# Compressed keys and values of a sparse attention: blocks stationary with 256 weight columns moving and a transpose of the result, instead of weight blocks stationary with 64 block columns moving

## The reference, cut to what matters

```python
def compress_blocks(t, tok, pos, w1, w2):
    B, _, G, dh = t.shape
    n_cmp, L = tok.shape
    blocks = t[:, tok] + pos[:, None, :].astype(t.dtype)
    flat = blocks.transpose(0, 1, 3, 2, 4).reshape(B, n_cmp, G, L * dh)
    return jax.nn.gelu(flat @ w1) @ w2
...
    n_cmp = (S - A_CMP_LEN) // A_CMP_STRIDE + 1
    tok = np.arange(n_cmp)[:, None] * A_CMP_STRIDE + np.arange(A_CMP_LEN)[None, :]
    k_cmp = compress_blocks(kc, tok, pos_k, w1_k, w2_k)
    v_cmp = compress_blocks(vc, tok, pos_v, w1_v, w2_v)
```

## Time and profile before

| | |
|---|---|
| median of 3 runs | 4209.5 us (4209.12 to 4214.65) |
| the profiled execution: its own time | 4212.07 us |
| its span in the profile | 4210.2 us |
| TensorE busy | 3891.7 us, 92% |
| VectorE busy | 2173.4 us, 52% |
| ScalarE busy | 1492.2 us, 35% |
| mean granted clock of TensorE | 0.962 |

### The profile page before, as it was taken

How to read it: one execution, slowest core, us unless ns; L and a number is a source line. 1 busy time by engine, 2 the same in 40 slices (tenths; PEclk the granted TensorE clock), 3 DMA queues, 4 the chain that set the end, 5 groups by cost and what they waited for, 6 DMA issues and landing times.

```text
span 4210.2 us, 52635 instructions
## 1 busy us (share of the span) xinstructions
PE 3891.7 (92%) x22400; PEld 3104.3 (74%) x22400; DVE 2173.4 (52%) x3113; ACT 1492.2 (35%) x2571; POOL 134.0 (3%) x160
## 2 busy tenths in 40 slices
PE   7978889879799999999988899999999979999998
PEld 4668658767587688787876687888777757878886
DVE  3764445464543447476545544534564555454346
ACT  3532223223422234343254523322433544232233
POOL 0122100010000000000000000000000000000000
PEclk8989999889899999999999999999999989999999
DMA  3100112103131122322300133333232001332322
GB/s 116 65 7 3 42 50 90 65 21 100 60 120 55 64 96 84 93 90 87 103 18 1 31 96 93 100 95 94 85 105 75 1 16 51 94 97 89 103 91 80
DMA packets 90815, 297.57 MB, mean 71 GB/s; under 512 B 10067, under 2 KB 12627, under 8 KB 90196
## 3 DMA queue, kind: packets, MB, share of 16 engines
q1 hardware_dynamic: 88704, 286.50, 21.4%
q10 hardware_dynamic: 1876, 7.71, 0.5%
HBM read 292.07 MB, written 2.10 MB: 70 GB/s over the span
## 4 chain that ended last, share of the span: by engine, by line
PE 78%; DVE 14%; ACT 5%; issue 2%; POOL 1%; DMA 0%; ACTq 0%; DVEq 0%
PE ps L616 19%; PE ps L617 19%; PE ps L618 19%; PE ps L1131 3%; PE ps L1153 3%; DVE wlo L1913 2%; ACT whi L1277 2%; PE ps L1144 2%; DVE ftm L1944 1%; PE ps L754 1%; PE ps L747 1%; PE ps L651 1%; PE ps L652 1%; PE ps L653 1%; PE ps L759 1%
## 5 line engine op out<-in xcount | busy, mean ns | idle before, releaser
L1913 DVE TENSOR_TENSOR wlo<-wraw,whi 128x1024 fp32r<-128x1024 f32 (+5 forms) x603 | 664.4, 1103 | 1434.1 <-ACT whi L1277 1429.2
L1277 ACT ACTIVATE whi<-wraw 128x1024 fp32r<-128x1024 f32 (+5 forms) x603 | 578.0, 959 | 1455.1 <-PE ps L618 1347.0
L616 PE MATMUL ps<-HH,whi 128*128 128x512 f32 x1816 | 724.0, 399 | 33.2 <-DVE wlo L1913 18.6
L617 PE MATMUL ps<-HL,whi 128*128 128x512 f32 x1816 | 710.7, 391 | 0.0
L618 PE MATMUL ps<-HH,wlo 128*128 128x512 f32 x1816 | 710.1, 391 | 0.0
L616 PEld LDWEIGHTS ps<-HH,whi 128*128 128x128 f32 x1816 | 343.0, 189 | 118.7 <-issue 25.3
L617 PEld LDWEIGHTS ps<-HL,whi 128*128 128x128 f32 x1816 | 343.1, 189 | 76.3 <-issue 6.3
L618 PEld LDWEIGHTS ps<-HH,wlo 128*128 128x128 f32 x1816 | 342.8, 189 | 72.8
L616 PE MATMUL ps<-HBh,whi 128*128 128x512 f32 x752 | 299.1, 398 | 6.9 <-DVE HBl L2414 6.4
L617 PE MATMUL ps<-HBl,whi 128*128 128x512 f32 x752 | 294.1, 391 | 0.0
L618 PE MATMUL ps<-HBh,wlo 128*128 128x512 f32 x752 | 293.6, 390 | 0.0
(11 more groups left out here) (604 smaller groups left out, 6731.4 us busy)
## 6 DMA issues: line engine op xcount, KB each, us to landing
wraw<-in_w_ff SPq DMA_DIRECT2D x88, 512.0 KB, 3.5
wraw<-in_w_bg SPq DMA_DIRECT2D x48, 512.0 KB, 3.5
wraw<-in_ffn_up SPq DMA_DIRECT2D x44, 512.0 KB, 3.3
wraw<-in_w_z SPq DMA_DIRECT2D x36, 512.0 KB, 3.3
wraw<-in_w_gate SPq DMA_DIRECT2D x32, 512.0 KB, 3.3
wraw<-in_w_br SPq DMA_DIRECT2D x32, 512.0 KB, 3.3
wraw<-in_w_rw SPq DMA_DIRECT2D x26, 512.0 KB, 3.3
wraw<-in_w_mam SPq DMA_DIRECT2D x24, 512.0 KB, 3.3
```

The costliest lines, as they stand in the source:

```text
L616: MM(b[0:m, :], hi[:, k, c0:c0 + m], x[0], start=(start and k == 0), stop=False)
L617: MM(b[0:m, :], hi[:, k, c0:c0 + m], x[1], start=False, stop=False)
L1277: ACTV(W.pair_of(n)[0], W.raw_of(n), ACT.Copy).then_inc(*up("act", "whi", n))
L1913: TT(l, W.raw_of(n), h.bitcast(F32), SUB).then_inc(*up("dve", "wlo", n))
```

## The change

The first product of the compression turns round. A piece of `KBh` or `KBl` is now the stationary operand and the 256 columns of a slot row of `w1` move, so a unit is 12 matmuls of 256 columns in place of 24 of 64 columns. A stationary piece is 128 columns wide, twice a slice of before: it takes in the next one as well, and the result rows 64 to 127 are not used. For that, the buffers get 64 more columns (1088). One PSUM bank collects the sum. It holds the hidden values with the blocks on 64 partitions, which is the wrong way round for the product with `w2`. So the GELU goes to a new tile `HT` (64x256), TensorE transposes it with two instructions in a step of its own, and ScalarE copies the result to `HD`. The steps per `n` are now 7 instead of 6, and the places where they come change from `j % 3` to `j % 5`: behind tiles 2, 3, 4, 6, 7, 8, 9, 11, 12, 13, 14, 16 and 17, and the last one after the loop.

```diff
@@ buffers
-                        KBp = (sb(c4, "KBh", 1024, dt=F32R), sb(c4, "KBl", 1024, dt=F32R))
-                        HD, W2 = sb(c4, "HD", 128), sb(c4, "W2", 256)
+                        KBp = (sb(c4, "KBh", 1088, dt=F32R), sb(c4, "KBl", 1088, dt=F32R))
+                        HT, HD, W2 = sb(c4, "HT", 256, 64), sb(c4, "HD", 128), sb(c4, "W2", 256)
@@
-        KBx = [YS[:, 0:1024], YSB[:, 0:1024]]
-        KB4x = [x.rearrange("p (l g n) -> p l g n", l=16, g=2) for x in KBx]
+        KBx = [YS[:, 0:1088], YSB[:, 0:1088]]
+        KB4x = [x[:, 0:1024].rearrange("p (l g n) -> p l g n", l=16, g=2) for x in KBx]
@@ compress, TensorE
-                    acc = [bank("kc", l, n, jt, hold=True) for jt in range(2)]
+                    acc = bank("kc", l, n, hold=True)
                     for lg in range(4):
                         w = W.take(("kc", l, n, lg), "w1" + "kv"[n], (l, lg), 4)
                         hi, lo = W.views(w)
                         for s in due("pe", ("dve", "wlo", w), ("dve", "kb", l, n)):
                             pe.wait_ge(*s)
-                        for jt in range(2):
-                            a = acc[jt]
-                            js = slice(128 * jt, 128 * jt + 128)
-                            for l4 in range(4):
-                                ks_ = slice(64 * (4 * lg + l4), 64 * (4 * lg + l4) + 64)
-                                first, end = lg == 0 and l4 == 0, lg == 3 and l4 == 3
-                                MM(a[:, 0:64], hi[:, l4, js], KBp[0][:, ks_], start=first, stop=False)
-                                MM(a[:, 0:64], hi[:, l4, js], KBp[1][:, ks_], start=False, stop=False)
-                                ins = MM(a[:, 0:64], lo[:, l4, js], KBp[0][:, ks_], start=False, stop=end)
-                            ins.then_inc(*up("pe", "kc", l, n, lg, jt))
+                        for l4 in range(4):
+                            k = slice(64 * (4 * lg + l4), 64 * (4 * lg + l4) + 128)
+                            first, end = lg == 0 and l4 == 0, lg == 3 and l4 == 3
+                            MM(acc[:, 0:256], KBp[0][:, k], hi[:, l4, :], start=first, stop=False)
+                            MM(acc[:, 0:256], KBp[1][:, k], hi[:, l4, :], start=False, stop=False)
+                            ins = MM(acc[:, 0:256], KBp[0][:, k], lo[:, l4, :], start=False, stop=end)
+                        ins.then_inc(*up("pe", "kc", l, n, lg))
                         here("pe", "w", w)
                         if lg < 3:
                             yield
-                    PS.let("kc", l, n, 0)
-                    PS.let("kc", l, n, 1)
+                    here("pe", "kc", l, n)
+                    PS.let("kc", l, n)
+                    yield
+                    b = bank("kct", l, n)
+                    for s in due("pe", ("act", "ht", l, n)):
+                        pe.wait_ge(*s)
+                    for jt in range(2):
+                        ins = TR(b[:, 64 * jt:64 * jt + 64], HT[:, 128 * jt:128 * jt + 128], C("ident")[0:64, 0:64])
+                    ins.then_inc(*up("pe", "kct", l, n))
                     yield
                     b = bank("kc2", l, n)
-                            hd = HD[:, 64 * g + 32 * jt:64 * g + 32 * jt + 31]
+                            hd = HD[:, 64 * jt + 32 * g:64 * jt + 32 * g + 31]
@@ z_proj, in the same way on TensorE, ScalarE and VectorE
-                    if j >= 2 and j % 3:
+                    if j >= 2 and j % 5:
                         next(steps, None)
@@ compress, ScalarE
-                    for jt in range(2):
-                        for need in due("act", ("pe", "kc", l, n, 3, jt), ("pe", "kc2", l, 0) if n else None):
-                            act.wait_ge(*need)
-                        ACTV(HD.rearrange("p (g j n) -> p g j n", g=2, j=2)[:, :, jt, :],
-                             r3(PS.of("kc", l, n, jt)[:, 0:64], 32),
-                             ACT.Gelu_apprx_tanh).then_inc(*up("act", "hd", l, n, jt))
-                        PS.free(("kc", l, n, jt), ("act", "hd", l, n, jt))
+                    evac(("kc", l, n), HT, ACT.Gelu_apprx_tanh, ("ht", l, n), rows=64, cols=256)
+                    yield
+                    for need in due("act", ("pe", "kc2", l, 0) if n else None):
+                        act.wait_ge(*need)
+                    evac(("kct", l, n), HD, ACT.Copy, ("hd", l, n), cols=128)
                     yield
                     yield
```

More of the change, by code:

```diff
@@ L1074, in compress @@
                             yield
-                    PS.let("kc", l, n, 0)
-                    PS.let("kc", l, n, 1)
+                    here("pe", "kc", l, n)
[7 more added lines that the diff above has]
+                    ins.then_inc(*up("pe", "kct", l, n))
                     yield
                     b = bank("kc2", l, n)
-                    for s in due("pe", ("act", "hd", l, n, 1), ("w2%d" % n, "ld", l)):
+                    for s in due("pe", ("act", "hd", l, n), ("w2%d" % n, "ld", l)):
                         pe.wait_ge(*s)
@@ L1297, in scaled_hi, with evac @@
                     ACTV(nm["outs"][j][0], sc[j % len(sc)], ACT.Copy).then_inc(*up("act", "hi", nm["tag"], j))
-            def evac(key, dst, fn, mark, **kw):
+            def evac(key, dst, fn, mark, rows=128, cols=S, **kw):
                 for need in due("act", ("pe", *key)):
                     act.wait_ge(*need)
-                ACTV(dst, PS.of(*key), fn, **kw).then_inc(*up("act", *mark))
+                ACTV(dst, PS.of(*key)[0:rows, 0:cols], fn, **kw).then_inc(*up("act", *mark))
                 PS.free(key, ("act", *mark))
@@ L2569, in compress @@
                     src, pname = ((kc, "poskT"), (vc, "posvT"))[n]
-                    for need in due("dve", OWN, ("pe", "kc", l, 0, 3, 1) if n else None):
+                    for need in due("dve", OWN, ("pe", "kc", l, 0, 3) if n else None):
                         dve.wait_ge(*need)
```

## The result

The changed kernel takes 4227.87 us (median; 4222.5 to 4228.4) against 4210.02 us for the kernel before on the same chip (4209.12 to 4214.65). The ratio is 1.0039, with a 95% interval of 1.0026 to 1.0052: it is slower by 17.9 us. The forecast was 4215.3 us, with a range of 4204 to 4226. The profiled execution of the changed kernel took 4227.89 us, span 4226.1 us, 15.9 us more than the span in the earlier trace rows, at a mean granted clock of 0.957 against 0.962.

A forecast was written before the change was run, and what follows sets the result against it. TensorE, busy 92% of the span, was taken as the bound. Terms -18.7 - 0.6 + 1.2 + 17.0 + 5.8 + 2.8 - 0.2 - 1.5 gave +5.8 us, so 4215.3 us against the median 4209.5; range 4204 to 4226.

The forecast's parts named there:

- Part 1: Compression units: 192 matmuls of 256 columns at 0.125 us replace 384 of 64 columns; saves 18.7 us, bounds 21.4 and 15.8.
- the rival of four passes: Compression matmuls: 256 columns exceed a limit of the format and take 0.43 us each; total 4274 us, chance 0.05.
- Part 2: Compression's four blocks: two added fp32 transposes each, with a ScalarE copy; +1.2 us, bounds 0.5 and 3.
- Part 3: First unit of each block: TensorE reaches it before VectorE has finished KBl and waits; +17.0 us in sum.
- The rival of no wait: First units: VectorE begins KBl 4 us or more earlier, so nothing waits for it; total 4192.5 us, chance 0.07.
- Part 4: Behind the four new waits for KBl: the granted clock falls, 1.45 us lost each; +5.8 us, bounds 0 and twice that.
- the clock part of 5: Projection tails: two shorter waits with dense work between give back a third of the old clock loss; -1.5 us, bounds 0 and -4.7.
- the rival of a clock that is low twice as long: Behind the waits for KBl: the clock loss doubles to 11.6 us; total 4221.1 us, chance 0.19.
- the rival of a clock that doesn't fall: Behind the waits for KBl: no clock loss; total 4209.5 us, no difference to be seen, chance 0.17.
- Part 5: Projection tails: tile 17 waits for the GELU through the freed bank, +2.8 us; last small product -0.2; clock -1.5.
- the handover: From a unit to the next projection tile: first matmul takes 0.23 us instead of 0.32, sixteen times; -0.6 us counted.

## Why the prediction was wrong

It got the sign right and the growth of the projections, and the total wrong by 12.6 us: it stopped at the end of the projection.

- **The sum for the stages that it covers held, in part by luck.** It forecast +5.8 us; the projections grew by 5.5. Single terms were off by up to 1.9 us, and these errors cancel.
- **Part 1, the wider matmuls.** 0.117 us each in place of 0.125: a unit is 1.41 us, and 16 x (2.67 - 1.41) = 20.2 us saved, within the bounds. One pass, so the rival of four passes is out. The Trainium skill ("TensorE: Matmul & The Clock Gate", Back-to-back issue gap) gives 0.109 for this; the measured value lies between that and the estimate from the rows.
- **Part 2, the transposes.** 0.27 us from the pair's start at 2034.05 to the next line, 1.1 us for four; forecast 1.2.
- **Part 3, the waits.** The starts of the units were right, the waits themselves not quite. For the keys of layer 0 the unit started 19.9 us behind the first swap, against 20.1 by the prediction. But the wait was 4.05 us and not 5.9, since TensorE came later: the first 6.2 us behind that swap ran at 0.50, while before the half clock ended after 2.8 us. That slow stretch cost nothing of its own, as the wait for VectorE hid it: its 1.7 us stand in the sum below in place of as much waiting. The others were 3.87, 2.79 and 3.87 us; 14.6 us in all, 16.3 with the 1.7, forecast 17.0. The rival of no wait is out.
- **Part 4 and the clock part of 5.** Forecast 5.8 and -1.5; by the half-clock rows 7.7 and -3.4, together 4.3 as forecast. The 7.7 us lie between the forecast and the rival of a clock that is low twice as long (11.6), and the rival of a clock that doesn't fall is out. At the tails, more came back than the third that the forecast gave them.
- **Part 5, the tail.** Tile 17 waited 1.30 us in each layer (2.6 us; forecast 2.8), and the last small product 0.93 in place of 1.30, a gain of 0.7 (forecast 0.2). The wait of `proj_tok` for `ZC`, 0.59 us in each layer (1.2 us), had no term.
- **The measured terms**: -20.2 + 1.1 + 14.6 + 1.7 + 7.7 - 3.4 + 2.6 - 0.7 + 1.2 - 0.2 (the old wait before the swap at 1992.77, gone) = +4.4 us. The other 1.1 us are not split: the handover, forecast at -0.6, was not measured apart, and the first matmul behind a wait takes longer (0.38 against 0.21 us at 1995.10).
- **The step that failed is the sum's last one**, which set the change of the projections equal to the change of the kernel. It had no term for stages behind the projection, and the range had none either. They added 7.9 us, mostly by stretches of half clock that the attention had not had before. The attention's own idle gaps (TensorE is busy 11.03 of 13.70 us in the stretch above) may be what leaves it open to that; no run took them away. The dense stages between (702.4 us) and behind (687.6 us) kept their times.

The stages explain 5.5 + 7.9 = 13.4 us; with a term of 7.9 us the forecast would have been 4223.2 us, inside its range. The medians differ by 17.9 us in the first comparison and by 10.6 in the second one of these two kernels. What lies between is the time ahead of the first swap, 1970.4 to 1975.2 us in the profiles, though no kernel here changes anything there, and the spread of the kernel before (4209 to 4222 us over the comparisons). What decides about it was not settled. Nor was it settled why a shift places the half-clock stretches as it does: a projection grown by 3.3 or 3.4 us left the attention alone, one grown by 3.7 us did not.

The twelve profiles do show where the added stretch comes. Every attention begins inside a stretch of half clock. First the kernel before, then the changed one, layer 0, from the first score matmul to the end of that stretch:

```profile
2124.08:2132.58 8.50, 7.14 (x28) 6.13 (x29) 3.71 (x13) 3.86 (x12) 0.00 (x0) 0.50 0.01 2
```

```profile
2131.01:2141.81 10.80, 9.44 (x40) 8.23 (x41) 4.81 (x17) 4.49 (x15) 0.00 (x0) 0.50 0.00 1
```

In 15 of the 24 attention stages (two layers, twelve profiles) it ended 8.4 to 9.9 us behind the first score matmul; none of them had another in the next 150 us, and they took 266.1 to 267.5 us. In the other nine it ended 10.8 to 11.8 us behind; all had another, 24.5 or some 35 us behind the first score matmul, and they took 268.6 to 272.7 us.

## What to carry to other kernels

Before an operand-bound step is moved one place forward, look up when its operand is finished: here the same matmuls at other places are worth 38.7 us (4186.7 against 4225.4 us on the same chip). An engine's wait costs the clock of what follows too, here another 8.6 us on 14.6 us of waits. And where a kernel has a later stage in which TensorE often idles, give the forecast a term of several microseconds for it, and compare changes stage by stage before a total is read as their worth. Here the term could only go up: the kernel before stood at the floor, as none of the 24 attention stages took less than 266.1 us.

## What the hardware showed that was not expected

- Identical instructions took 266.2 to 272.7 us in the attention of layer 0, depending on what happened in the projection ahead of it: 266.2 us (granted clock 0.94) in the kernel before, 271.8 us (0.91) in the changed one. A delay of 2.6 us cost 7.6, one of 3.4 us cost 3.4, and 2.1 us of added work shortened the attention by 5.3 us.
- The Trainium skill ("TensorE: Matmul & The Clock Gate", What's actually happening) says that the number of matmuls that run at half clock varies with the phase at the kernel's start, and puts the penalty of the ramp under 1% of a typical kernel. It speaks of the start of a kernel, and what moved here lies in its middle; the size is under that bound too, 5.6 us or 0.13% of the span. But it is as much as the whole net effect of this change in its own stages.
- Fp32r matmuls start 0.111 us apart with 64 columns and 0.117 us with 256 in this kernel: four times the columns for 5% more time. In both the stationary block changes with every matmul.
